# Splitting half of the SSD branch's raw products, and giving expert 6 three quarters of a buffer in former descriptor space

## The reference

```python
h = rms_norm(x, norm1_g); z, xbc, dt, q, k, v, g_ssd, g_att = split(h @ w_in)
y_ssd = ssd_branch(z, xbc, dt, ...) @ w_ssd_out        # 512x2048 @ 2048x1024: "the branch"
y_att = swa_sink_branch(q, k, v, ...) @ w_attn_out
x = x + (sigmoid(g_ssd) * y_ssd + sigmoid(g_att) * y_att) @ w_out
h2 = rms_norm(x, norm2_g)
# 64 experts, 2 for each token: hid = silu(xb @ w_gate[e]) * (xb @ w_up[e]); hid @ w_down[e]
return x + hier_moe(h2, ...)
```

## Time and profile before

| | |
|---|---|
| median of 3 runs | 2058.34 us (2056.51 to 2059.31) |
| profiled execution | 2059.48 us, its span 2057.6 us |
| TensorE busy | 1983.6 us (96%), mean granted clock 0.988 |
| VectorE, ScalarE, GpSimd busy | 1004.9, 746.5, 221.3 us |
| DMA | 379.89 MB; share 42.7% of 16 engines' span in queue 1 (SyncE's), 5.3% in queue 0 (GpSimd's) |

### The profile page before, as it was taken

One profiled execution on the slowest core, in us unless ns is written; L12 is line 12 of the kernel. 1 busy time (PEld: TensorE's weight loads), 2 busy tenths in 40 slices (PEclk: granted clock), 3 DMA queues, 4 the chain that ended last, 5 costly groups with the idle time before them and its releaser, 6 DMA issues.

```text
span 2057.6 us, 23256 instructions
## 1 busy us (share of the span) xinstructions
PE 1983.6 (96%) x9524; PEld 1409.8 (69%) x9524; DVE 1004.9 (49%) x1599; ACT 746.5 (36%) x1283; POOL 221.3 (11%) x271
## 2 busy tenths in 40 slices
PE   7999999999999999999999999999999998898888
PEld 6877788888888888887888776678886332233223
DVE  4376533445766642568888738664434211111113
ACT  5353332234444431456555533662333111111111
POOL 2000000002000000202111113110011221111110
PEclk9999999999999999999999999999999999999999
DMA  7231222243222242323333221112387999999998
GB/s 267 103 123 62 82 83 82 103 153 124 103 103 95 90 143 103 133 84 108 128 118 104 85 103 62 43 65 99 106 323 300 418 410 422 422 425 422 423 425 340
DMA packets 60602, 379.89 MB, mean 185 GB/s; under 512 B 13240, under 2 KB 13496, under 8 KB 28624
## 3 DMA queue, kind: packets, MB, share of 16 engines
q1 hardware_dynamic: 42336, 339.23, 42.7%
q0 software_dynamic: 17584, 38.09, 5.3%
q10 hardware_dynamic: 576, 1.09, 0.2%
HBM read 377.80 MB, written 27.89 MB: 197 GB/s over the span
## 4 chain that ended last, share of the span: by engine, by line
PE 77%; DMA 13%; DVE 6%; ACT 2%; POOL 1%; issue 1%; SPq 0%; DVEq 0%; ACTq 0%
PE PS L523 18%; PE PS L525 18%; PE PS L524 18%; DMA AR<-in_wexp 12%; PE PS L1290 7%; PE PS L984 3%; PE PS L1318 3%; DMA AR<-x2d 1%; PE PS L889 1%; DVE AR L1720 1%; PE PS L1036 1%; PE PS L1066 1%; POOL AR L2841 1%; DVE rf L1346 1%; PE PS L1054 1%
## 5 line engine op out<-in xcount | busy, mean ns | idle before, releaser
L523 PE MATMUL PS<-rf,rf 128*128 128x512 f32 (+1 forms) x1944 | 751.9, 387 | 5.4 <-DVE rf L1346 5.4
L525 PE MATMUL PS<-rf,rf 128*128 128x512 f32 (+1 forms) x1944 | 740.8, 381 | 0.0
L524 PE MATMUL PS<-rf,rf 128*128 128x512 f32 (+1 forms) x1944 | 740.5, 381 | 0.0
L1346 DVE TENSOR_TENSOR rf<-AR,rf 128x1024 fp32r<-128x1024 f32 (+1 forms) x228 | 286.0, 1260 | 334.4 <-ACT rf L2277 334.4
L523 PEld LDWEIGHTS PS<-rf,rf 128*128 128x128 f32 x1944 | 365.9, 188 | 81.7 <-DVE rf L1346 7.3
L525 PEld LDWEIGHTS PS<-rf,rf 128*128 128x128 f32 x1944 | 365.9, 188 | 70.9
L524 PEld LDWEIGHTS PS<-rf,rf 128*128 128x128 f32 x1944 | 366.2, 188 | 68.6 <-issue 1.2
L2277 ACT ACTIVATE rf<-AR 128x1024 fp32r<-128x1024 f32 (+1 forms) x228 | 245.3, 1084 | 257.4 <-PE PS L525 202.7
L1290 PE MATMUL PS<-AR 128*64 128x512 f32 x1024 | 264.9, 633 | 29.8 <-DMA AR<-in_wexp 29.8
L1290 PEld LDWEIGHTS PS<-AR 128*64 128x64 f32 x1024 | 81.3, 145 | 207.4 <-issue 159.4
L2219 DVE TENSOR_TENSOR AR<-AR,PS 128x256 f32<-128x256 f32 x31 | 13.1, 421 | 321.5 <-ACT AR L2830 321.5
(11 more groups left out here) (347 smaller groups left out, 1810.2 us busy)
## 6 DMA issues: line engine op xcount, KB each, us to landing
AR<-in_wpack SPq DMA_DIRECT2D x123, 1024.0 KB, 5.0
AR<-in_wexp SPq DMA_DIRECT2D x52, 2048.0 KB, 34.9
AR<-in_wexp SPq DMA_DIRECT2D x70, 1024.0 KB, 34.9
AR<-in_wexp SPq DMA_DIRECT2D x36, 512.0 KB, 8.8
AR<-acud POOLq DMA_DIRECT2D x16, 512.0 KB, 4.9
AR<-ya SPq DMA_DIRECT2D x4, 1024.0 KB, 7.8
bvec<-bv POOLq DMA_DIRECT2D x1, 2560.0 KB, 15.9
AR<-in_x SPq DMA_DIRECT2D x4, 512.0 KB, 7.7
```

The costliest lines, as they stand in the source:

```text
L523: e.i.matmul(o, ws[0], xs[0], start=start, stop=False)
L524: e.i.matmul(o, ws[0], xs[1], start=False, stop=False)
L525: return e.i.matmul(o, ws[1], xs[0], start=False, stop=stop)
L1346: e.i.tensor_tensor(rounded(p.place + p.width, p.width), src, rounded(p.place, p.width).bitcast(F32), ALU.subtract).then_inc(*tick("w_lo", ...
```

## The change

**Branch tiles 0 to 4.** Half of each tile's products (d = 0 to 7) are now split, the other half stays raw. `raw_tile` becomes `branch_tile`; chunks of kind "r" become kind "h", with one part of 1024 columns. YH[0] to YH[7] and YL[0] to YL[7] are made before the q0 rows are taken from the accumulators. YH[0] to YH[5] lie in EX, six tiles in 3072 columns. The parts of gates and branch get an order of their own.

```diff
-        if c.kind != "r":
+        if c.kind == "h":
+            c.parts = [Part((c.name, 2 * c.half), c, 0, 1024)]
+        else:
...
+        elif c.name == "gs0" and c.half == 0:
...
+            parts += [g0, s0, g1, g2, s1, g3, s2, g4, s3, g5, s4, g6, g7]
...
+            def branch_tile(k, u):
+                slot, j = f"so{k // 2}", 2 * (k % 2)
                 if u == 0:
                     b, was = banks.take(("so", k), ("v_out", ("gm2", k)), own[1])
                     e.wait_ge(*at(*was))
...
+                    for d in range(8):
+                        e.wait_ge(*at("v_out", ("yl", d)))
+                        m = product(PS[:, b, :], (wh[:, d, :], wl[:, d, :]), (YH[d], YL[d]), d == 0, False)
+                    m.then_inc(*tick("w_read", (slot, j)))
+                    return
...
+                for d in range(8, 16):
+                    m = e.i.matmul(PS[:, b, :], w[:, d, :], YT[:, d, :], start=False, stop=d == 15)
```

The calls in `dense_2`, here ScalarE's (VectorE's `ahead3` stand at the same steps), where `ahead3(n)` goes up to part n of the list, counted from g0:

```diff
             def dense_2():
-                ahead2("gs0", 0, 2)
-                yield
+                ahead3(3)
+                yield
+                ahead3(4)
                 gate_s(0)
                 yield
-                yield
-                ahead2("gs0", 1, 2)
+                ahead3(5)
+                yield
                 yield
                 gate_s(1)
-                ahead2("gs0", 2, 2)
+                ahead3(6)
                 gate_s(2)
                 yield
                 for k in range(1, 5):
...
+                    ahead3((7, 9, 11, 13)[k - 1])
+                    yield
+                    if k < 4:
+                        ahead3((8, 10, 12)[k - 1])
+                    yield
+                    yield
+                    gate_s(k + 2)
```

```diff
+        EX = ctx.enter_context(nc.sbuf_tensor("EX", [128, 3072], F32))
...
+        def gate_cols(n, lo, hi):
+            o = GUs[n % 6]
+            if n % 2 == 0 and 6 <= n < 60 and lo < 3072:
+                if n == 6:
+                    return EX[:, lo:hi]
+                o = GUs[(n - 2) % 6]
+            return area(o + lo, hi - lo)
```

```diff
+            e.wait_ge(*at("acc", ("so", 7)))
+            first_in(6)
+            for blk in range(3, END - 1):
                 n, m = 2 * blk, 2 * blk + 1
                 if blk < 6:
                     e.wait_ge(*at("acc", ("gu_half", blk - 3)))
-                    for x in (n, m):
-                        expert_in(f"gu{x % 6}", (x, "half"), x, area(GUs[x % 6], 2048), 0)
+                    expert_in(f"gu{m % 6}", (m, "half"), m, gate_cols(m, 0, 2048), 0)
                     e.wait_ge(*at("acc", ("gu", blk - 3)))
-                    for x in (n, m):
-                        expert_in(f"gu{x % 6}", x, x, area(GUs[x % 6] + 2048, 2048), 2048)
+                    rest_in(n, 3072)
+                    rest_in(m, 2048)
+                    first_in(n + 2)
                 else:
-                    gates_in(n)
-                    gates_in(m)
...
+                    e.wait_ge(*at("acc", ("gu", blk - 3)))
+                    if blk > 6:
+                        first_in(n)
+                    rest_in(n, 3072)
+                    rest_in(m, 0)
                 downs_in(n)
                 downs_in(m)
+            n, m = 2 * END - 2, 2 * END - 1
+            e.wait_ge(*at("acc", ("gu", END - 4)))
+            rest_in(m, 0)
+            e.wait_ge(*at("acc", ("gu", END - 3)))
+            rest_in(n, 0)
...
+            expert_in(f"gu{m % 6}", m, m, gate_cols(m, 0, 2048), 0)
+            e.wait_ge(*at("acc", ("gu", END - 2)))
```

**The first two blocks on TensorE** (VectorE and ScalarE follow suit; on VectorE `over` comes before `hidden_out(0)`, `over_slots` before `rows_out(1)`):

```diff
+            gates(0)
+            first_scales()
+            weights()
+            turned_rows(1)
+            gates(1)
+            hidden(0)
+            turned_rows(2)
+            downs(0)
+            hidden(1)
+            downs(1)
+            for blk in range(2, NBLK):
...
+                gates(blk)
+                if blk + 1 < NBLK:
+                    turned_rows(blk + 1)
+                hidden(blk)
+                downs(blk)
```

More of the change, by code:

```diff
@@ L132, in weight_plan @@
             parts += [a, y, b, z]
-        elif c.name[:2] not in ("ga", "gb", "gc", "gt"):
+        elif c.name == "gs0" and c.half == 0:
+            (g0, g1), (g2, g3), (g4, g5), (g6, g7) = (out_of[n, h] for n in ("gs0", "gs1") for h in range(2))
+            s0, s1, s2, s3, s4 = (out_of[f"so{k // 2}", k % 2][0] for k in range(5))
+            parts += [g0, s0, g1, g2, s1, g3, s2, g4, s3, g5, s4, g6, g7]
+        elif c.name[:2] not in ("ga", "gb", "gc", "gt", "gs") and c.kind != "h":
             parts += c.parts
@@ L293, in two_layers @@
         spots += [(p.place + p.width * i, p.width) for p in parts for i in range(2)] + [(WRo + 22528, 4096), (WRo + 26624, 4096)]
+        EXo = 52624
+        spots += [(EXo + 512 * i, 512) for i in range(6)]
         RF = {}
@@ L1270, in turned_rows, with gates @@
                     m.then_inc(*tick("acc", ("xt", blk, hf)))
-            banks.i += (bs[3, 0] - banks.i) % 8
-            for blk in range(NBLK):
-                s = blk % 2
-                xt, hs, hd = cut(XT[:, s, :], 8), HS[:, s, :], cut(HD[:, s, :], 2)
-                if blk == END:
-                    overflow(e, tensor_more, before_end)
+            def gates(blk):
+                xt = cut(XT[:, blk % 2, :], 8)
                 b, was = banks.take(("gu", blk), ("v_out", ("hm", blk)))
@@ L1294, in tensor, with hidden @@
                 m.then_inc(*tick("acc", ("gu", blk)))
-                if blk == 0:
-                    first_scales()
-                    weights()
-                if blk + 1 < NBLK:
-                    turned_rows(blk + 1)
+            def hidden(blk):
+                s = blk % 2
                 b, was = banks.take(("ht", blk), ("v_out", ("hd", blk)))
@@ L1816, in vector, with branch_low @@
                 ahead("q0", u)
+            def branch_low(d):
+                e.wait_ge(*at("a_out", ("yh", d)))
+                if d > 7:
+                    e.wait_ge(*at("acc", ("so", 4)))
+                e.i.tensor_tensor(YL[d], YT[:, d, :], YH[d].bitcast(F32), ALU.subtract).then_inc(*tick("v_out", ("yl", d)))
+            for d in range(8):
+                branch_low(d)
             turned_at = ("acc", ("yt", 3, 3))
@@ L1855, in ahead2, with ahead3 @@
                 lows.upto(e, min(PART[name, j] + n, PART["oo0", 0]))
+            def ahead3(n):
+                lows.upto(e, PART["gs0", 0] + n)
             def gated_rows(k):
@@ L1994, in vector @@
             ahead2("so2", 2, 2)
-            for d in range(8, 16):
+            for d in range(12, 16):
                 branch_low(d)
@@ new lines, in vector @@
+            e.wait_ge(*at("acc", "rs0"))
+            e.i.tensor_copy(col("rs0", 1), ps("rs0")[:, 0:1]).then_inc(*tick("v_out", "rs0"))
+            e.wait_ge(*at("a_out", ("hs", 0)))
+            e.i.scalar_tensor_tensor(out=HS[:, 0, :], in0=ps(("gu", 0))[:, 256:512], scalar=col("rs0", 1), in1=HS[:, 0, :],
+                                     op0=ALU.mult, op1=ALU.mult).then_inc(*tick("v_out", ("hm", 0)))
+            turned_rows(1)
+            e.wait_ge(*at("acc", "wts"))
+            e.i.tensor_copy(wts, ps("wts")[:, 0:1]).then_inc(*tick("v_out", "wts"))
@@ L2212, in vector @@
+            over()
+            hidden_out(0)
+            hidden(1)
+            turned_rows(2)
+            rows_out(0)
+            hidden_out(1)
+            over_slots()
+            rows_out(1)
+            for blk in range(2, NBLK):
                 if blk == END:
                     overflow(e, vector_more, before_end)
-                e.wait_ge(*at("a_out", ("hs", blk)))
-                if blk == 0:
-                    e.i.scalar_tensor_tensor(out=hs, in0=ps(("gu", 0))[:, 256:512], scalar=col("rs0", 1), in1=hs, op0=ALU.mult,
-                                             op1=ALU.mult).then_inc(*tick("v_out", ("hm", 0)))
-                else:
-                    e.i.tensor_tensor(hs, hs, ps(("gu", blk))[:, 256:512], ALU.mult).then_inc(*tick("v_out", ("hm", blk)))
+                hidden(blk)
@@ L2616, in scalar, with branch_high @@
                     turn(3, 3)
+            def branch_high(d):
+                if d > 5:
+                    e.wait_ge(*at(*YH_AT[d - 6][1]))
+                e.wait_ge(*at("a_out", ("yt", 3, 3)))
+                e.i.activation(YH[d], YT[:, d, :], ACT.Copy).then_inc(*tick("a_out", ("yh", d)))
+            for d in range(8):
+                branch_high(d)
             for s, name in enumerate(("q0", "q1")):
```

202 lines of the change are left out of this document (99 added, 103 removed).

## The result

| | before (same chip and session) | changed |
|---|---|---|
| median | 2057.43 us (2055.16 to 2059.31, 4 runs) | 2071.41 us (2070.85 to 2072.79, 4 runs) |
| profiled execution, its span | 2059.48, 2057.6 us | 2070.85, 2069.0 us |

The ratio is 1.0066 with a 95% interval of 1.0053 to 1.0078: slower, by 14 us. I had put 2061.3, with 2052 to 2067 as the range, so the time fell outside it. The two profiled executions are only 11.4 us apart: the one before lies 2.1 us over its median, the changed one 0.6 under.

A forecast was written before the change was run, and what follows sets the result against it. Bounds taken: dense TensorE work ahead of 1504, DMA loads of expert weights until 2016, then TensorE alone for 41 us. Terms -2.9 + 4.2 + 1.7 = +3.0 on the 2058.34 median made 2061.3 us, range 2052 to 2067.

The forecast's parts named there:

- 1, fewer passes: Branch tiles 0 to 4: eight split products take 5.44 us instead of 6.87 raw, 7.15 us less over five tiles.
- 2, the other engines: Dense part: conversions cost 0 in the loop over k; late rotary loses the first tile's 1.43 us and 2.85 more.
- Branch total: Dense part: -7.15 + 1.43 + 2.85 = -2.9 us, bounds -7.15 and +0.5.
- 3, 1.5 MB ahead: Start of expert stage: loading expert 6's 3072 columns into EX early fills the first DMA hole, -3.7 us.
- 4, gates(1) before downs(0): Expert blocks 0 and 1: block 0's down products end 7.9 us later, delaying expert 6's down weights; with part 3, +4.2.
- 5, smaller pieces: Blocks 3 to 29: 27 new 512 KB loads from the 3072 + 1024 split cost +1.7 us, bounds 0 and 3.4.
- 6, last blocks: End of expert stage: new waits ahead of experts 60 and 62 open no hole; last 41 us stay, 0.
- A: Expert-load queue isn't starved by the later down products: 2053.4 us, faster; chance 0.22.
- B: Before the q and k transposes: squares' delay is absorbed, TensorE starts them when ready: 2057.1 us; chance 0.12.
- C: TensorE stays at the lower clock in gates(1), 1581 to 1595: 2066.0 us, slower; chance 0.21.
- D: The smaller descriptor ring makes the kernel slower; chance 0.04.
- E: Expert loads: each added issue costs a fixed time, 27 x 3.7 = 100 us, 2160 us; chance 0.01.

The follow-up runs named there:

- three_orders: Changed kernel with rot_first's moves, one conversion for each step of the loop over k, and ScalarE's sigmoid behind the copies of tt2: 2062.02 us, +3.1.
- rot_first: Changed kernel with the conversions before the rotary put behind squares and sums, or into VectorE's pause: 2068.28 us, +10.1.
- low_later: Changed kernel with the gate part's high and low a step later in the loop over k, as in the kernel before: 2068.92 us, +10.7.
- ex6_only: Kernel before with 3072 gate columns of expert 6 loaded early into EX and the smaller descriptor ring, orders as before: 2058.36 us, -0.5.
- moe_downs_first: moe_only with downs(0) ahead of gates(1) again, as in the kernel before: 2057.97 us, +0.1.
- moe_only: Kernel before with only the change's expert half (early 3072-column loads, gates(1) before downs(0)) and the smaller ring: 2064.66 us, +6.5.
- ring_only: Kernel before with nothing but the smaller descriptor ring (dynamic_dma_scratch_size 4096): 2058.03 us, -0.9.
- orders_downs: three_orders with downs(0) ahead of gates(1) again; all that the change computes and loads is kept: 2056.19 us, -1.7.
- best: Dense part of three_orders, and of the expert half only expert 6's 3072 columns in EX: 2055.83 us, -2.0.
- downs_first: Changed kernel with downs(0) ahead of gates(1) again, VectorE's and ScalarE's orders of blocks 0 and 1 to match: 2064.22 us, +5.3.
- dense_only: Kernel before with only the change's dense half (split branch halves, conversion order, YH in EX) and the smaller ring: 2067.16 us, +9.0.

## Why the prediction was wrong

**1, fewer passes: right in kind, a fifth too high.** A split half takes 5.8 us from start to start, not 5.44: in the half from 1267.80 on, products lie 0.70 us apart and not 0.68, the first and the last take 0.8; a raw half took 6.96 to 7.07, not 6.87. So each of the four tiles in the loop saves 1.1 to 1.3 us instead of 1.43: 4.7 of 5.7 us, and 4.8 where nothing else is late (three_orders). Part 1 named "none of it, if the other engines are late" as a bound, but the range did not use it.

**2, the other engines: the step that failed.** It has two parts.

The rotary chain was followed correctly: squares behind g1's high, a low ahead of sums 2 and 3, rotary end forecast at 1257.7 and measured at 1258.2, a wait of 4.00 us. The kv rows end 0.8 us later as well, which I had at 0. What I left out is TensorE's clock, which stood at 0.50 behind the wait. The transposes took 2.7 us more at it than the 4.26 of rot_first at 1.00. That kernel shows wait and low clock going together, and so does its own wait of 2.55 us in the loop. In part 4 I had priced a lower clock, yet not here, where the forecast itself made TensorE idle.

"In the loop over k these lie beside attention with room to spare: 0 each" was wrong, and is the largest miss: 5.7 us forecast, nothing measured. Of the 5.7, 1.0 is part 1's error and 4.5 are TensorE's new waits. I compared busy times (VectorE and ScalarE are far from full) where the question was the order in a ring that closes once for each pair of heads. Two things in it: the gate part's low had moved a step forward, ahead of gated rows and shares, and waits there for a high made behind both exps (3.32 us of idle VectorE at 1286.4); low_later takes that out for 2.3 us of TensorE. And ScalarE's chain from scores to copies was already nearly as long as TensorE's work beside it. Rows of the kernel before, ScalarE and TensorE:

```profile
1293.96 1.85 ACT L2727 ACTIVATE AR<-PS 128x384 f32<-128x384 f32 x4
```
```profile
1296.41 1.75 PE L1066 MATMUL PS<-AR 128*64 128x128 f32 x28
```

In the changed kernel, where the products wait for the copies, they start 1.90 us after these do (1301.83 in ScalarE's timeline, 1303.73 in TensorE's). By that the copies were through at 1295.86 before, 0.55 us ahead of need. A branch half shortened by 1.13 us takes more than that cover away: TensorE waits 0.66 us, and the table load and sigmoid lie on the path. Putting the sigmoid behind the copies gives 2.5 more. Branch total: -2.9 forecast, +6.65 measured at block 0's gates.

**3, 1.5 MB ahead: not a gain by itself.** The hole was filled, and the -3.7 counted that as time won. In ex6_only, with the load into EX and the orders of before, the hole ahead of that wait was only moved: the second hole took 4 us for 2.8, and the time was 0.5 us less. The bytes that count are those ahead of that wait in SyncE's order. In the changed kernel these are 1.5 MB more, as `first_in(8)` stands there too, and with the -3.7 the terms of its trace add up: +5.4 for the release, -3.7, +3.0 by the rates are the measured +4.7. The median of moe_downs_first shows no such gain, so its worth there stays open.

**4, gates(1) before downs(0): right.** +7.9 forecast for the release of the down buffers; +5.4 in the trace, +8.5 between moe_only and moe_downs_first, and 6.4 us in their times. The clock in gates(1) was at 1.00 in the changed kernel, so my half clock for 4.5 us, the 0.51 up to 1585.3 of rows 2, did not come there; in moe_only it came in part (7.81 us instead of 7.09 for the gates), and in low_later in full: 9.21 us for the 9.2 forecast. That the forecast took the clock of one trace for that of all was the weak spot of this part: the kernel before has it at 0.51 in one trace, ring_only at 1.00.

**5, smaller pieces: +1.7 forecast**, 2.0 to 3.0 by the rates of 419 and 418 GB/s, not seen in orders_downs against best. Unsettled within the intervals. **6, last blocks:** 0 forecast; the tail is 0.6 us longer.

**The rivals.** A asked for a queue that isn't starved: it was, more than before. B asked for transposes on time: they were 4 us late. GpSimd's power (L2844) did take 3.56 us beside a VectorE that waited for most of it and 4.49 to 4.51 beside a busy one in the trace of before, but its four took 3.56, 4.51, 4.49 and 4.49 us in the changed kernel as well; in rot_first they took the same, with VectorE busy for 2.2 us of the 3.56, so the waits of VectorE alone don't explain the shorter one. C's low clock in gates(1) didn't come in the changed kernel; it did in low_later. A kernel made slower by the smaller ring, the 0.04 given to D, is refuted by ring_only (-0.9 us), E by the rate of 418 GB/s with 63 issues of 512 KB, where there were 36. None had the loop: no rival questioned the "0 each", and the range had no room for it. With -5.7 set to 0 and the 3.4 us by which the first scores came later than forecast, the prediction's +3.0 becomes 12.1; the expert stage gave back 1.2 (+4.7 for +5.9), which leaves 10.9, and the spans differ by 11.4. That the expert stage comes within 1.2 us of its forecast is in part luck: the release came 2.5 us less late than forecast, since the trace of before has the low clock there, and the rate cost 1.3 us more.

## What to carry to other kernels

Where work is taken from the engine that bounds, it was also the cover of every chain that runs beside it (here 4.7 us of work went and 4.5 us of waits came): take the chain from its last input to the instruction that the bounding engine waits for, engine by engine in queue order, and compare it with the work that is left beside it, not with busy shares. An operation that is moved forward in an engine's order holds back what stands behind it, also when it only waits: the low of the gate part waited 3.32 us at 1286.4 in the changed kernel, with gated rows and shares behind it. Filling an idle stretch of the DMA engines ahead of a wait whose release did not move gave -0.5 us in ex6_only, which is no change that shows, and not the -3.7 forecast; count the bytes that pass before that release.

## What the runs showed of the hardware

TensorE's granted clock fell during or just after the wait of 4.00 us ahead of the transposes of q and k, in all four traces that have it: in the changed kernel and in downs_first to 0.50 for nearly all 37 transposes, which took 6.96 and 6.78 us, in dense_only and low_later to 0.51 and 0.53 for the first of them (5.65 and 5.86 us). After a wait of 1.38 us (rot_first) it stayed at 1.00, and they took 4.26 us. After a wait of 2.55 us in the loop of the same trace it fell to 0.50; after waits of 1.41 and 1.81 us in the changed kernel's loop it stayed at 1.00. In the changed kernel it read 1.00 from 1256 to 1257 and 0.50 from 1257 to 1258, with no matmul running, and 1.00 again from 1264 to 1265, with the transposes running.

The same sequence of small matmuls ahead of block 1 (40 of one column, then transposes) was followed by a granted clock of 0.51 for 6.8 us before, of 0.76 for 7 us in moe_only, of 0.50 for 6 us in low_later (1584 to 1590), and of 1.00 in the changed kernel, in moe_downs_first and in ring_only, whose matmuls are those of before. Such a phase can't be forecast from one trace; it should stand in the range, not in the sum.
